# Decoder step on one core: the feed-forward's Strassen-like units interleaved in pairs, two units by plain products, GpSimd's additions on VectorE

## The reference, cut to what matters

```python
def finish_layer(x, a_heads, m_out, lam_init, attn_out_norm, w_out, norm_ffn, w_up, w_down):
    ...
    x = x + jnp.concatenate([a, m_out], axis=-1) @ w_out
    hf = rms_norm(x, norm_ffn) @ w_up
    return x + jnp.square(jax.nn.relu(hf)) @ w_down
```

## Time and profile before

| | |
|---|---|
| three executions | 3689.84, 3693.04, 3695.39 us, median 3693.04 |
| the profiled execution | 3696.58 us, its span 3694.9 us |
| TensorE matmul busy | 3404.5 us (92%), 24702 matmuls |
| VectorE busy | 2250.3 us (61%) |
| ScalarE busy | 1643.3 us (44%) |
| GpSimd busy | 913.5 us (25%) |
| granted TensorE clock, mean | 0.951 |
| feed-forward | from about 2228 us to the end of the span |

### The profile page before, as it was taken

The page is one execution under the profiler, slowest core; times in us unless marked ns, Lnnn a source line. Parts: engine busy times, 40 slices in busy tenths (PEclk is TensorE's granted clock), DMA queues, the critical chain, the costliest instruction groups (busy, mean ns, idle before and its releaser), DMA issues. The chain is left out here.

```text
span 3694.9 us, 64011 instructions
## 1 busy us (share of the span) xinstructions
PE 3404.5 (92%) x24702; PEld 3148.9 (85%) x24702; DVE 2250.3 (61%) x3124; ACT 1643.3 (44%) x2478; POOL 913.5 (25%) x592
## 2 busy tenths in 40 slices
PE   7999998886787999999997997999999999999999
PEld 7999998554645888888885996999999999999998
DVE  4222222774447777777776328677777777777775
ACT  3111110343122887787775214545545544443443
POOL 0000000000000888888883003211211111111100
PEclk9999999877877999999997998999999999999999
DMA  8444441305825999999996522454454656464643
GB/s 216 107 112 107 111 109 59 108 1 169 221 79 192 338 332 330 341 328 328 338 332 194 171 81 82 135 158 143 138 161 137 218 157 220 146 224 141 224 135 95
DMA packets 480085, 666.63 MB, mean 180 GB/s; under 512 B 44098, under 2 KB 367856, under 8 KB 476212
## 3 DMA queue, kind: packets, MB, share of 16 engines
q1 hardware_dynamic: 479796, 662.69, 55.9%
HBM read 567.10 MB, written 95.52 MB: 179 GB/s over the span
## 5 line engine op out<-in xcount | busy, mean ns | idle before, releaser
L69 PE MATMUL ff_acc<-ff_xhi,ff_wlo 128*128 128x272 f32 x3568 | 1047.3, 294 | 65.8 <-DVE ff_wlo L2748 27.9
L71 PE MATMUL ff_acc<-ff_xhi,ff_whi 128*128 128x272 f32 x3568 | 1041.6, 292 | 0.0
L70 PE MATMUL ff_acc<-ff_xlo,ff_whi 128*128 128x272 f32 x3568 | 1036.8, 291 | 0.0
L69 PEld LDWEIGHTS ff_acc<-ff_xhi,ff_wlo 128*128 128x128 f32 x3568 | 681.3, 191 | 71.8 <-DVE ff_wlo L2748 30.5
L70 PEld LDWEIGHTS ff_acc<-ff_xlo,ff_whi 128*128 128x128 f32 x3568 | 682.5, 191 | 0.0
L71 PEld LDWEIGHTS ff_acc<-ff_xhi,ff_whi 128*128 128x128 f32 x3568 | 680.9, 191 | 0.0
L1695 POOL TENSOR_TENSOR dc_vl<-dc_vpages,dc_vh 128x1024 fp32r<-128x1024 f32 x241 | 573.7, 2395 | 12.4 <-ACT dc_vh L2034 12.0
L69 PE MATMUL z_acc<-xn_hi,win_lo 128*128 128x280 f32 (+1 forms) x1536 | 446.2, 290 | 1.1 <-DVE win_lo L303 1.1
L71 PE MATMUL z_acc<-xn_hi,win_hi 128*128 128x280 f32 (+1 forms) x1536 | 446.7, 291 | 0.0
L70 PE MATMUL z_acc<-xn_lo,win_hi 128*128 128x280 f32 (+1 forms) x1536 | 445.4, 290 | 0.0
L1875 DVE TENSOR_TENSOR dc_kl<-dc_pk,dc_kh 128x512 fp32r<-128x512 f32 x512 | 337.9, 681 | 175.7 <-ACT dc_kh L2034 175.3
(11 more groups left out here) (414 smaller groups left out, 5967.2 us busy)
## 6 DMA issues: line engine op xcount, KB each, us to landing
dc_kpages<-in_cache_k SPq DMA_DIRECT2D x256, 512.0 KB, 5.3
dc_vpages<-in_cache_v SPq DMA_DIRECT2D x256, 512.0 KB, 5.1
win_raw<-in_w_in SPq DMA_DIRECT2D x48, 1024.0 KB, 6.3
ffn_raw<-in_w_up SPq DMA_DIRECT2D x34, 1024.0 KB, 7.2
mix_t<-in_w_down SPq DMA_DIRECT2D x32, 1024.0 KB, 6.8
ffn_raw<-in_w_down SPq DMA_DIRECT2D x32, 1024.0 KB, 6.9
mix_t<-in_w_up SPq DMA_DIRECT2D x30, 1024.0 KB, 7.1
ff_xlo<-hq_scratch SPq DMA_DIRECT2D x28, 1088.0 KB, 13.7
```

Source lines behind the costliest of these rows:

```text
L69: nc.tensor.matmul(out, wlo, xhi, start=first, stop=False, skip_group_check=resumed)
L70: nc.tensor.matmul(out, whi, xlo, start=False, stop=False, skip_group_check=resumed)
L71: return nc.tensor.matmul(out, whi, xhi, start=False, stop=last, skip_group_check=resumed)
```

## The change

In the order of the program:

- `mean_square` of half 0 moves from after k-slice 11 to after k-slice 7 of the last tile's second half.
- Units 0 and 1 both go by plain products (8 block products each, 192 matmuls each); ScalarE's `take_plain` copies their results out.
- Units 2 to 61 go in pairs: step i of the even unit, then step i of the odd unit, then step i+1 of the even one. The 14 steps of a pair are called its slots 0 to 13 here; steps are counted from the stage's start, so step 8 is slot 0 of units 2 and 3. Units 62 and 63 go one after the other. `held` has two halves, one for each unit of a pair.
- The sum buffer `ff_s1` is gone; `sum1` is made in place, and all four sums of a unit are made around its own steps 1, 2 and 3. No sum is made a unit ahead.
- GpSimd has no block in this stage. Its start sums, combinations (`combine`, three instructions for four) and additions (`finish` for all 32 down units) are VectorE's.
- The loops of each engine are over g, the step in the new order, and each piece of work stands a fixed number of steps behind the step it follows: holds 3, joins 3, `finish` 5, `combine` 6, the operand loads 3, their high parts 7, their remainders 8.
- Of the final transposes' results the prompt part goes through a buffer `ff_y`.

```diff
@@ finish_and_project
-                    if last and h == 1 and k == 3 * d.kc // 4 - 1:
+                    if last and h == 1 and k == d.kc // 2 - 1:
                         mean_square(pe, 0)
@@ feed_forward
-    step = lambda u, i: i if u == 0 else FIRST + STEPS * (u - 1) + turns(u).index(i)
+    order = [(u, i) for u in range(PLAIN) for i in range(4)]
+    for p in range(PLAIN, UNITS - 2, 2):
+        order += [(p + f, i) for i in range(STEPS) for f in range(2)]
+    order += [(u, i) for u in (UNITS - 2, UNITS - 1) for i in range(STEPS)]
+    G = len(order)
...
-        total = sb("ff_s1", [P, KH, P])
-        held = sb("ff_held", [P, 3, H])
+        held = sb("ff_held", [P, 2, 3, H])
+        ystage = sb("ff_y", [P, 2, 512])
...
+            for u, v, count in ((1, 0, 2), (1, 1, 4), (2, 0, 6), (2, 1, 8)):
+                sp.wait_ge(lo_made, count)
+                weights(u, v)
+            sp.wait_ge(t_lo, 4)
+            weights(3, 0)
+            weights(3, 1)
+            for g in range(4 * PLAIN, G + 3):
+                u, i = at(g)
+                if i == 4 and u + 2 < UNITS:
+                    sp.wait_ge(lo_made, g + 1)
+                    weights(u + 2, 0)
+                if i == 6 and u + 2 < UNITS:
+                    sp.wait_ge(lo_made, g + 1)
+                    weights(u + 2, 1)
+                u, i = at(g - 3)
+                if last_of_block(u) and i >= 0:
+                    operand(u, i)
...
-        @block.gpsimd
-        def _(pool):
...
+            def take_plain(u):
+                free_piece(act, u)
+                act.wait_ge(used, 4 * u + 4)
+                for m, x in enumerate((*acc[u], extra[1 - u])):
+                    A(piece(u)[:, m, :], x[:, 0:H]).then_inc(out_taken, 1)
...
+            high(4)
+            high(5)
+            high_t(3, xn(0, 1), 2)
+            high(6)
+            high_t(2, xn(0, 0), 3)
+            high(7)
+            high_t(4, xn(1, 1), 1)
+            high(8)
+            high_t(6, last_t, 4)
+            take_plain(0)
+            for g in range(9, G + 3):
+                if g < G:
+                    high(g)
+                if g == 9:
+                    relu_square(0)
+                if g == 10:
+                    take_plain(1)
...
+            dve.wait_ge(x_lo, d.kc)
+            V.tensor_tensor(xn(1, 1), xn(1, 1), xn(0, 1), ALU.subtract).then_inc(t_made, 1)
+            dve.wait_ge(t_made, 1)
+            V.tensor_tensor(xn(0, 1), xn(0, 1), xn(0, 0), ALU.subtract).then_inc(t_made, 1)
+            low(6)
...
+            for g in range(9, G + 5):
+                u, i = at(g - 3)
+                if i == 3:
+                    join(u, 0, 0, 1, 1, s1, c11)
...
+                u, i = at(g - 5)
+                if i == 6 and u >= PAIRS:
+                    finish(u)
...
+                u, i = at(g - 6)
+                if i == 6 and u < PAIRS:
+                    combine(u)
+                u, i = at(g - 8)
+                if last_of_block(u) and i >= 0:
+                    op_low(u, i)
+                if g < G:
+                    low(g)
+                u, i = at(g)
+                if i == 1:
+                    sum1(u)
+                    sum2(u)
+                if i == 2:
+                    sum4(u)
+                if i == 3:
+                    sum3(u)
...
+                if i in (0, 1, 3):
+                    if nth(u) < 3:
+                        pe.wait_ge(out_taken, 4 * (u - 1))
```

More of the change, by code:

```diff
@@ L2407 @@
 STEPS = 7
+PLAIN = 2
 HQ = (0, 1, 4, 3, 5, 2, 6)
@@ L2431, in feed_forward @@
     UNITS, LAST = 2 * PAIRS, 2 * PAIRS - OUTS
-    FIRST = 4
-    assert PAIRS == 4 * OUTS and KH == 8 and 2 * H == d.to
-    turns = lambda u: (0, 1, 3, 2, 4, 5, 6) if u == 1 else tuple(range(STEPS))
-    step = lambda u, i: i if u == 0 else FIRST + STEPS * (u - 1) + turns(u).index(i)
+    assert PAIRS == 4 * OUTS and KH == 8 and 2 * H == d.to and OUTS % 2 == 0 and PLAIN == 2
+    order = [(u, i) for u in range(PLAIN) for i in range(4)]
[3 more added lines that the diff above has]
+    G = len(order)
+    place_of = {x: g for g, x in enumerate(order)}
+    step = lambda u, i: place_of[u, i]
+    at = lambda g: order[g] if 4 * PLAIN <= g < G else (-1, -1)
+    nth = lambda u: u - PLAIN + 1
     with ExitStack() as ctx:
@@ L2507, in weights, with keep_h @@
                 sp.dma_start(slot(u, v).rearrange("p (k n) -> p k n", n=2 * P), w).then_inc(landed[base(u) + v], 16)
-            def more(u, v):
-                if u >= 1 and u + 2 < UNITS:
-                    sp.wait_ge(lo_made, step(u, 4 if v == 0 else 6) + 1)
-                    weights(u + 2, v)
-            def keep_hidden(u):
-                sp.wait_ge(combined, 4 * u + 4)
+            def keep_h(u):
+                sp.wait_ge(combined, 3 * u + 3)
                 x, b = piece(u), u // OUTS
@@ L2625, in _ @@
+            send(UNITS - 2)
+            send(UNITS - 1)
+            for r in range(3):
+                sp.wait_ge(y_stored[r], 16 * OUTS)
         @block.scalar
@@ L2743, in _, with low @@
             V = nc.vector
-            def low(u, i):
-                g = step(u, i)
+            def low(g):
+                u, i = order[g]
                 dve.wait_ge(hi_made, g + 1)
@@ L2843, in _ @@
-            join(UNITS - 1, 3, 2, 0, 4, s5, c22)
-            join(UNITS - 1, 1, 1, 2, 5, s2, c12)
-            finish(UNITS - 1)
+                    low((0, 4, 6).index(k) + 1)
+            low(4)
+            low(5)
+            dve.wait_ge(x_lo, d.kc)
[3 more added lines that the diff above has]
+            low(6)
+            dve.wait_ge(t_made, 2)
@@ new lines, in _ @@
+                if i in (2, 4, 5):
+                    pe.wait_ge({2: s1, 4: s2, 5: s5}[i], nth(u))
+                if i == 6:
+                    pe.wait_ge(c22, nth(u))
+                out = b[(0, 1, 0, 2, 0, 2, 0)[i]][:, 0:H]
+                for k in range(KH):
+                    mm = exact_passes(nc, out, wh(g)[:, k, :], wl(g)[:, k, :], xh[:, i, k, :], xl[:, i, k, :],
+                                      k == 0 and i in (0, 1, 3), k == KH - 1, i not in (0, 1, 3))
+                mm.then_inc(used, 1)
@@ L2910, in output_shapes @@
+            turn(UNITS - 2, 2)
+            for e in range(3):
+                turn(UNITS - 1, e)
 def output_shapes(a):
```

434 lines of the change are left out of this document (174 added, 260 removed).

## The result

The changed kernel takes **3676.1 us** (median of 7 runs, 3671.5 to 3684.1), against 3693.0 of the kernel before (7 runs beside them): ratio 0.995, 95% interval 0.9938 to 0.9961, so 14 to 23 us faster. Forecast were 3656 and a gain of 37.4. The direction is right, the gain a little under half of the forecast, and the range (3640 to 3677) barely holds the median.

What follows compares the result with a forecast made beforehand. TensorE was full in steady units, with time lost at the four changes of block (57.3 us) and the start. Terms -9.5 + 1.7 + 5 - 36.3 + 1.7 = -37.4 took 3693.0 to 3656 us, range 3640 to 3677.

Steps and rivals of the forecast that it cites:

- Mean square: Stage ahead: `mean_square` four k-slices earlier lets VectorE's last addition start about 1.1 us earlier; gain 1.1 us.
- Start: Plain units to step 9: GpSimd's silence gives more than all, unit 3's late load takes back; gain 9.5 us.
- Its four terms for ScalarE: Before step 9: a copy 1.0, relu and square 2.2, a copy 1.0, four copies out 1.2; given as 5.5.
- The gap: Before step 9: about 8 us near 2292 to 2300, halving the clock for about 3 us; loss 1.7.
- Crowding in up pairs: VectorE's queue in slots 2 to 5 ends 0.3 to 0.4 us late in 14 up pairs; loss 5 us.
- Changes of block: Four changes of block: 21.0 us lost instead of 57.3; gain 36.3 us.
- so the loads stop being the bound. VectorE is: At changes, each load has four slots, 12 us; VectorE's remainders run up to 5.0 us late, 6.0 at the first.
- The rival "loads still late": At changes, operands take 13.7 us and ScalarE's waiting delays weights' copies: +20, 3676 us; chance 0.12.
- The clock term of 1.7: One clock fall at the first change of block; loss 1.7 us.
- `ff_y` for the results: End of the stage: the results' new buffer costs nothing, units 62 and 63 in sequence, transposes as before.
- Weights late in every pair: Second half of weights landing beyond 9.8 us is paid in 30 pairs; 3722 at 12 us; chance 0.05.

Runs made afterwards that it cites:

- the traces of before: Kernel before, profiled, profiled again, and with mean_square alone moved: stage 1487.3, 1487.4 and 1482.4 us.
- the units one by one: Kernel before with GpSimd's work given to VectorE, no pairs, one plain unit: 3693.3 us against 3694.5.
- the start's edit: Changed kernel, last activation sum made in its own place, unit 3's weights loaded earlier, unit 1's results copied out before step 9's weights: 3673.2 us.
- the run with GpSimd back: Changed kernel with combine and finish given back to GpSimd, start sums staying on VectorE: 3710.3 us.
- the small remainders: Changed kernel with VectorE's 28 operand remainders made for the first 272 of 2176 columns only; results not the reference's: 3660.7 us.
- the small loads: Changed kernel with the 28 operand loads cut to the first 272 of 2176 columns; results not the reference's: 3669.7 us.
- The early sends: Changed kernel with the two prompt transfers of `ff_y` issued 2 steps earlier in the SP queue: 3665.9 us.
- the run with the finish later: Changed kernel with `finish` of units 32 to 55 at 10 steps instead of 5, next running result loaded at 12: 3720.5 us.

## Why the prediction was half right

- **Mean square:** -0.8 for -1.1. Right.
- **Start:** -8.3 for -6.7 with the clock (-7.6 to -9.9 over the traces of before). Right in mechanism and place: the units one by one show that GpSimd's silence makes it, and the start's edit shows the late load and the late copy-out, together, as what ended it. Its four terms for ScalarE add up to 5.4 and not 5.5, which changes nothing. The gap did halve the clock: 0.50 from 2300.4 to 2303.4.
- **Crowding in up pairs:** +1.3, mostly in the first pair (43.92 us), for +5. The term was mis-sized, with the mechanism right. The forecast put the end of slot 5's remainder at 15.45 us of the pair against 15.13 needed. VectorE's timeline and TensorE's first matmul of slot 5:

```profile
2512.64 1.23 DVE L2715 TENSOR_TENSOR ff_wlo<-ffn_raw,ff_whi 128x1024 fp32r<-128x1024 f32 x1 [1.80 <-ACT ff_whi L2588]
...
2525.15 1.22 DVE L2715 TENSOR_TENSOR ff_wlo<-mix_t,ff_whi 128x1024 fp32r<-128x1024 f32 x1
```

```profile
2526.48 0.35 PE L69 MATMUL ff_acc<-ff_xhi,ff_wlo 128*128 128x272 f32 x1
```

  The first row is slot 2's remainder, the second slot 5's. From the start of the one to the end of the other it is 13.73 us and not 14.08: a combine takes 1.59, not 1.72, and a pair of sums 2.40, not 2.47. The end, 2526.37, is 0.1 us ahead of the matmul that needs it, so the pair takes 42.42 against 42.38 before. The forecast saw how near it was; the run with GpSimd back shows what falling over that edge costs, 1.4 us a pair.
- **Changes of block:** the step "so the loads stop being the bound. VectorE is" failed by half. The extras behind the changes were 21.7 us for 21.0, and the small remainders take 16.8 of them away: right. But the loads still cost 9.5 us ahead of the changes, shown by the small loads. The forecast gave each load four slots and checked only its own landing; it didn't ask what the queue does to the weights behind it. The rival "loads still late" had ScalarE waiting for the operands and the weights' copies held up behind that; it was priced at 20 and came to 9.5. Over the traces of before the row came out 7.6 to 10.9 us short of the forecast. The clock term of 1.7 was not needed.
- **The end:** the step that costed "`ff_y` for the results" at nothing failed, and is the largest error, 12.2 us. It looked at the order of the transposes and not at who may overwrite the buffer, nor where its transfer stands in the queue. The same text had asked that question of `weights` and answered it well. The early sends give back 11.4. No rival and no sign of being wrong pointed here.
- **Weights late in every pair** didn't happen: 1.00 clock and no wait in steady pairs. In the run with the finish later, a load in front of the weights made it happen.
- **The range:** it held the median by luck. Its upper end was made for loads that cost 20 us; they cost 9.5, and a wait that the forecast had at nothing filled the room, while start and up units came out 5 us better.

## What to carry to other kernels

When an edit puts a new small buffer between two engines and a DMA, find the issue's place in its queue and everything it waits behind, before costing the buffer at nothing: single buffering was fine with the issue 10 us earlier. Count a burst of transfers against every transfer that shares its stretch, above all the small-margin one behind it, not only against its own due time. And two edits can be worthless or harmful alone and good together: GpSimd's work moved gave nothing that the runs can tell (ratio 0.9985 to 1.001; 8.5 us in the stage's trace), the pairs with GpSimd lost 16, both together gained 17.

## What the runs showed of the hardware

The clock's fall doesn't follow from the length of the wait alone. Windows of the changed kernel, each beginning at the end of a wait of 2.91 us:

```profile
2957.70:2960.70 3.00, 2.99 (x23) 2.99 (x24) 2.90 (x3) 0.00 (x0) 0.00 (x0) 1.00 0.07 22
3550.50:3553.50 3.00, 3.00 (x15) 2.99 (x16) 1.48 (x2) 2.97 (x5) 0.00 (x0) 0.51 0.78 193
```

After the first the granted clock is 1.00, that is 2.4 GHz, after the second about 0.5, 1.2 GHz. The Trainium skill, "TensorE: Matmul & The Clock Gate", section "HAM oscillation — how this bites in real kernels", has idle gaps that put the clock down again each time, in a kernel whose waits are of some 3 to 5 us. No gap at a change of block did so in the changed kernel, and both waits at the end did. In the kernel before, a gap of 2.66 us (to 3507.01) was enough: 0.50 in the 3 us behind it. What decides between them stays open.

Issuing a DMA can itself take long. The operand's issue at 3280.53 holds the SP queue for 5.24 us, where weights take 0.37 and an operand's issue 11 us earlier 0.58. The DMA share is 1.03 in that stretch:

```profile
3280.53:3285.77 5.24, 5.24 (x44) 5.24 (x43) 3.98 (x4) 3.68 (x3) 0.00 (x0) 1.00 1.03 384
```

That full DMA engines are the reason is likely and not shown: no run varies it alone.
